# Moving half of the modulation products and the gate broadcasts of a two-layer diffusion block into the stretches between its projections

## What is computed

```python
for l in range(2):
    sh1, sc1, gt1, sh2, sc2, gt2 = split(silu(c) @ w_mod[l] + b_mod[l], 6)      # w_mod[l]: 1024 x 6144
    csh1, csc1, cgt1, csh2, csc2, cgt2 = the same of c_ctx
    h = rms_norm(x, g_pre_mix[l]) * (1 + sc1) + sh1                             # hc likewise for ctx
    y, yc = token_mixer(h, hc, ...)       # @ w_in; differential attention; gated linear attention; @ w_out
    x = x + gt1 * rms_norm(y, g_post_mix[l])                                    # ctx too, in layer 0
    h = rms_norm(x, g_pre_ffn[l]) * (1 + sc2) + sh2
    x = x + gt2 * rms_norm(ffn(h), g_post_ffn[l])   # layer 0: dense SwiGLU, layer 1: 8 experts, top 2
```

## Time and profile before

| | |
|---|---|
| median of 3 runs | 2058.43 us (2058.36 to 2059.71) |
| the profiled execution's own time | 2058.17 us |
| its span | 2056.0 us |
| PE busy, DVE, ACT | 93%, 60%, 52% of the span |
| DMA | 441.87 MB, 215 GB/s on average |

### The profile page before, as it was taken

One profiled execution on the slowest core, in us unless ns is written; L12 is line 12 of the kernel. 1 busy time (PEld: TensorE's weight loads), 2 busy tenths in 40 slices (PEclk: granted clock), 3 DMA queues, 4 the chain that ended last, 5 costly groups with the idle time before them and its releaser, 6 DMA issues.

```text
span 2056.0 us, 25790 instructions
## 1 busy us (share of the span) xinstructions
PE 1911.4 (93%) x10392; PEld 1579.1 (77%) x10392; DVE 1243.5 (60%) x1379; ACT 1069.3 (52%) x1368; POOL 43.6 (2%) x38
## 2 busy tenths in 40 slices
PE   6999889979999998898887999999999999999995
PEld 4889456868888786788567788888888888888784
DVE  3241751452222334442654889898989898888886
ACT  4232642352222224433534677677777777676764
POOL 0000000000000000000000020000000000000000
PEclk9999885889999999899967899999999999999997
DMA  8211633212222222212802899998989998989894
GB/s 336 103 62 63 226 145 121 73 49 105 83 103 102 82 103 82 89 62 103 307 22 82 319 350 368 338 368 343 366 342 364 344 362 346 360 343 343 336 339 163
DMA packets 61530, 441.87 MB, mean 215 GB/s; under 512 B 6836, under 2 KB 6964, under 8 KB 8288
## 3 DMA queue, kind: packets, MB, share of 16 engines
q1 hardware_dynamic: 60032, 436.23, 56.3%
q10 hardware_dynamic: 1120, 3.28, 0.4%
q0 software_dynamic: 256, 0.66, 0.1%
HBM read 439.10 MB, written 1.05 MB: 214 GB/s over the span
## 4 chain that ended last, share of the span: by engine, by line
PE 84%; DVE 10%; ACT 3%; DMA 2%; issue 1%; SPq 0%; DVEq 0%; ACTq 0%
PE psum L1446 72%; DMA raw<-units 2%; PE psum L1782 2%; PE psum L1658 1%; PE psum L1664 1%; DVE act_lo L1088 1%; PE psum L1641 1%; PE psum L1825 1%; DVE row_max L1168 1%; PE psum L1463 1%; PE psum L1798 1%; ACT probs L773 1%; DVE states L1199 1%; PE psum L1469 1%; DVE y_mix L1237 1%
## 5 line engine op out<-in xcount | busy, mean ns | idle before, releaser
L1331 DVE TENSOR_TENSOR w_lo<-raw,w_hi 128x2048 fp32r<-128x2048 f32 x136 | 311.0, 2289 | 52.3 <-ACT w_hi L922 51.6
L922 ACT ACTIVATE w_hi<-raw 128x2048 fp32r<-128x2048 f32 x136 | 260.8, 1919 | 109.0 <-PE psum L1446 106.4
L1024 DVE TENSOR_TENSOR w_lo<-raw,w_hi 128x1024 fp32r<-128x1024 f32 x130 | 153.3, 1221 | 197.9 <-ACT w_hi L628 197.9
L1446 PE MATMUL psum<-w_hi,xt_hi 128*128 128x512 f32 x596 | 234.2, 393 | 2.7 <-DVE xt_lo L1336 2.7
L1446 PE MATMUL psum<-w_hi,xt_lo 128*128 128x512 f32 x596 | 233.4, 392 | 0.0
L1446 PE MATMUL psum<-w_lo,xt_hi 128*128 128x512 f32 x596 | 233.2, 391 | 0.0
L1331 DVE TENSOR_TENSOR w_lo<-raw_more,w_hi 128x2048 fp32r<-128x2048 f32 x90 | 206.0, 2290 | 35.7 <-ACT w_hi L922 35.3
L628 ACT ACTIVATE w_hi<-raw 128x1024 fp32r<-128x1024 f32 x130 | 130.2, 1051 | 157.2 <-PE psum L1446 151.6
L922 ACT ACTIVATE w_hi<-raw_more 128x2048 fp32r<-128x2048 f32 x90 | 172.8, 1920 | 75.4 <-PE psum L1446 75.4
L1446 PE MATMUL psum<-act_hi,w_hi 128*128 128x512 f32 (+1 forms) x544 | 208.8, 384 | 2.1 <-DVE act_lo L1088 1.9
L1446 PE MATMUL psum<-act_lo,w_hi 128*128 128x512 f32 (+1 forms) x544 | 207.6, 382 | 0.0
(11 more groups left out here) (260 smaller groups left out, 3636.1 us busy)
## 6 DMA issues: line engine op xcount, KB each, us to landing
raw<-units SPq DMA_DIRECT2D x295, 1024.0 KB, 4.9
raw_more<-units SPq DMA_DIRECT2D x120, 1024.0 KB, 4.9
X<-ctx_in ACTq DMA_DIRECT2D x1, 1024.0 KB, 16.6
X<-x_in ACTq DMA_DIRECT2D x1, 1024.0 KB, 23.3
out<-X SPq DMA_DIRECT2D x1, 1024.0 KB, 4.1
const<-const_in ACTq DMA_DIRECT2D x1, 520.0 KB, 9.6
rope<-rope_in POOLq DMA_DIRECT2D x2, 256.0 KB, 5.6
wsm<-wsm_in ACTq DMA_DIRECT2D x1, 288.0 KB, 26.9
```

Of the source, the lines that this page charges most:

```text
L922: act.activation(w_place(m)[0], raw_place(m), ACT.Copy).then_inc(esem("w_high"), 1)
L1024: ins = dve.tensor_tensor(w_lo[:, i % RING, part], raw[:, i % RING, part], w_hi[:, i % RING, part].bitcast(F32), ALU.subtract)
L1331: dve.tensor_tensor(lo, raw_place(m), hi.bitcast(F32), ALU.subtract).then_inc(esem("w_ready"), 1)
L1446: ins = pe.matmul(dst, lhs(a), rhs(b), start=first and n == 0, stop=last and n == 2)
```

## The change

The 48 modulation units keep their order by need, but 24 of them leave attention and GLA. Of layer 0's attention, units 20 to 23 go; units 0 to 7 of layer 1 leave GLA; all twelve go into the gap before the dense FFN. Of layer 1's attention, units 8 to 15 go into the gap before its input projection and units 20 to 23 into the gap after its output projection; units 16 to 19 stay, now with one step every item. `gap_places` lists the places in a gap: P (after a tile's squares of y), N (after a tile's squares of X), V, and, before the dense FFN only in effect, K (after column blocks 1, 3, 5, 7 of `modulated`). PE does the steps of the P, N and V places before the turn, those of K after the eight T jobs. Two projection units (`AHEAD`) are numbered before a gap's modulation units. The gate broadcasts w=0 move from before the output projection to behind it, those of w=1 to the end of the dense FFN (layer 0) and behind the turn (layer 1). The DVE split of the first output unit now falls into attention, as do ACT's splits of the first two. `residual` runs tile by tile with steps between, one tile behind the squares after a mixer and two behind after the FFN.

```diff
+MOD_GROUPS = {
+    ("mod_a", 0): [(0, j) for j in range(MOD_A)],
+    ("mod_att", 0): [(0, j) for j in range(MOD_A, 20)],
+    ("mod_ffn", 0): [(0, j) for j in range(20, MOD_UNITS)] + [(1, j) for j in range(MOD_A)],
+    ("mod_mix", 1): [(1, j) for j in range(MOD_A, 16)],
+    ("mod_att", 1): [(1, j) for j in range(16, 20)],
+    ("mod_ffn", 1): [(1, j) for j in range(20, MOD_UNITS)],
+}
+AHEAD = 2
+STAGES = (("mod_a", 0), ("in", 0), ("mod_att", 0), ("out", 0), ("up_ahead", 0), ("mod_ffn", 0), ("up", 0), ("down", 0),
+          ("in_ahead", 1), ("mod_mix", 1), ("in", 1), ("mod_att", 1), ("out", 1), ("mod_ffn", 1), ("moe", 1))
...
 def beside(l, stage):
-    if (l, stage) == (1, "gla"):
-        return {}
-    units, step = {(0, "att"): ([(0, j) for j in range(MOD_A, MOD_UNITS)], 2),
-                   (1, "att"): ([(1, j) for j in range(MOD_A, MOD_UNITS)], 1),
-                   (0, "gla"): ([(1, j) for j in range(MOD_A)], 2)}[l, stage]
-    return {n * step: here for n, here in enumerate(mod_steps(units))}
+    return {2 * n: here for n, here in enumerate(mod_steps(MOD_GROUPS["mod_" + stage, l]))}
+def gap_places(l, stage):
+    tiles = len(token_tiles(l, stage))
+    places = [("P", n) for n in range(tiles)] + [("N", n) for n in range(tiles)] + [("V", 0)]
+    places += [("K", k) for k in (1, 3, 5, 7)]
+    return dict(zip(places, mod_steps(MOD_GROUPS["mod_" + stage, l])))
+def gap_jobs(l, stage, behind):
+    return [key for place, here in gap_places(l, stage).items() if (place[0] == "K") == behind for key in here]
...
 # ACT, out_projection
+            gates_on_all(l, 0)
             act.wait_ge(sem(f"act_lo_out{l}"), KT)
-            mean_square("post", l, "mix", ...)
-            gates_on_all(l, 1)
+            for n in range(len(token_tiles(l, "out"))):
+                mean_square("post", l, "mix", ..., (n,))
+                gap(l, "ffn", ("P", n))
+        def normed(l, stage):
+            for n in range(len(token_tiles(l, stage))):
+                norm(l, stage, (n,))
+                gap(l, stage, ("N", n))
+            gap(l, stage, ("V", 0))
 # ACT, end of dense_ffn
             for t in range(TILES):
                 for h in range(2):
                     key = ("D", 0, t, h)
                     copy_out(key, y_ffn[:, t, h * 512:(h + 1) * 512], bank(key))
...
+                if t == 1:
+                    gates_on_all(0, 1)
+                if t:
+                    tile_square(t - 1)
+            tile_square(TILES - 1)
+            for n in range(TILES):
+                gap(1, "mix", ("P", n))
...
 # DVE
+        def residual_beside(l, stage, y, after):
+            tiles = len(token_tiles(l, "out"))
+            behind = 1 if stage == "mix" else 2
+            for n in range(tiles + behind):
+                if n >= behind:
+                    residual(l, stage, y, n - behind)
+                if n < tiles and stage == "mix":
+                    gap(*after, ("P", n))
+                elif stage != "mix" and n >= 2:
+                    gap(*after, ("P", n - 2))
+        def normed(l, stage):
+            for n in range(len(token_tiles(l, stage))):
+                gap(l, stage, ("N", n))
+                norm(l, stage, (n,))
+            gap(l, stage, ("V", 0))
...
 # PE
+            if l == 1:
+                gates_on_all(0, 1)
+                for key in gap_jobs(1, "mix", False):
+                    mod_step(*key)
             turn(l, "mix")
...
             gla(l)
+            out_projection(l)
             gates_on_all(l, 0)
-            out_projection(l)
-            gates_on_all(l, 1)
+            for key in gap_jobs(l, "ffn", False):
+                mod_step(*key)
             turn(l, "ffn")
+            for key in gap_jobs(l, "ffn", True):
+                mod_step(*key)
             if l == 0:
                 dense_ffn()
...
+        gates_on_all(1, 1)
         for q in range(4):
             key, tt = ("H2", q), q // 2
```

More of the change, by code:

```diff
@@ L60 @@
 EXPERT_UNITS = 3 * FC
[L64 to L67, removed]
+MOD_GROUPS = {
[9 more added lines that the diff above has]
+          ("in_ahead", 1), ("mod_mix", 1), ("in", 1), ("mod_att", 1), ("out", 1), ("mod_ffn", 1), ("moe", 1))
+STAGE_UNITS = {("in", 0): IN_F + IN_K, ("out", 0): OUT_UNITS, ("up_ahead", 0): AHEAD, ("up", 0): UP_UNITS - AHEAD,
+               ("down", 0): DOWN_UNITS, ("in_ahead", 1): AHEAD, ("in", 1): IN_F + IN_K - AHEAD, ("out", 1): OUT_UNITS,
+               ("moe", 1): EXPERTS * EXPERT_UNITS}
+STAGE_UNITS.update({stage: len(here) for stage, here in MOD_GROUPS.items()})
 def unit_numbers():
@@ L85, in split_numbers @@
     for stage in STAGES:
-        for i in range(STAGE_UNITS[stage[0]]):
-            if stage[0] not in ("mod_a", "mod_b"):
+        for i in range(STAGE_UNITS[stage]):
+            if stage not in MOD_GROUPS:
                 at[U[stage] + i] = n
@@ L110, in mod_unit, with in_unit, up_unit @@
 def mod_unit(l, j):
-    return U["mod_a", l] + j if j < MOD_A else U["mod_b", l] + j - MOD_A
+    return next(U[stage] + here.index((l, j)) for stage, here in MOD_GROUPS.items() if (l, j) in here)
+def in_unit(l, u):
+    return U["in", 0] + u if l == 0 else U["in_ahead", 1] + u if u < AHEAD else U["in", 1] + u - AHEAD
+def up_unit(j):
+    return U["up_ahead", 0] + j if j < AHEAD else U["up", 0] + j - AHEAD
 def mod_steps(units):
@@ L211, in psum_jobs @@
             out += [key for here in mod_steps([(0, j) for j in range(MOD_A)]) for key in here]
+        if l == 1:
+            out += [("GB", 0, 1, s, h) for s in sides(0) for h in range(2)]
+            out += gap_jobs(1, "mix", False)
         out += [("T", l, "mix", k) for k in range(KT)]
+        out += gap_jobs(1, "mix", True) if l == 1 else []
         out += [("F", l, f) for f in range(2 * IN_F)]
@@ L249, in psum_jobs @@
         else:
+            out += [("GB", 1, 1, s, h) for s in sides(1) for h in range(2)]
             out += [("H2", q) for q in range(4)] + [("LG",), ("POS",)]
@@ L658, in beside_item, with gap @@
                 mod_step(*key)
+        def gap(l, stage, place):
+            for key in gap_places(l, stage).get(place, ()):
+                mod_step(*key, ahead=0)
         def gates_on_all(l, w):
@@ L868, in dense_ffn, with tile_copied, tile_square @@
                 act.activation(ffn_hi[:, f % 2, :], ffnT[:, f, :], ACT.Copy).then_inc(sem("ffn_hi"), 1)
+            def tile_copied(n):
+                for h in range(2):
+                    wait_copied(act, ("D", 0, n, h))
+            def tile_square(t):
+                mean_square("post", 0, "ffn", range(TILES), y_ffn_of, lambda t: y_junk[:, :], tile_copied, (t,))
             for t in range(TILES):
@@ L1089, in low_parts @@
                                   ALU.subtract).then_inc(sem(f"act_lo_{stage}{l}"), 1)
+                if stage != "out" and (l, stage) != (0, "mix"):
+                    gap(l, stage, ("K", k))
         def in_projection(l):
@@ L1437, in _ @@
         dve.wait_ge(sem("summed"), 1)
-        residual(1, "ffn", y_moe_of)
+        for n in range(2):
+            residual(1, "ffn", y_moe_of, n)
     @block.tensor
```

113 lines of the change are left out of this document (54 added, 59 removed).

## The result

The kernel after takes 2073.47 us (median of 4 runs, 2072.95 to 2074.01) beside 2059.07 (4 runs, 2058.36 to 2062.63) for the kernel before on the same chip: ratio 1.0066, 95% interval 1.0049 to 1.0084. It is slower. The traces are compared by span, 2071.8 against 2056.0: 15.8 us to explain.

The account below looks back on a forecast made before the run. PE carried 84% of the chain of waits, but the five changed places had different limits. Against 2058.17 us: -18.9 + 1.7 + 15 + 15.5 - 11.8 + 0 + 5.5 = +7.0, 2065.2 us; range 2049 to 2077.

Parts of the forecast that it names:

- GLA 0: Layer 0's GLA loses eight modulation steps and falls from 70.2 to 51.3 us: -18.9 us.
- the first gap to its turn: Gap before the dense FFN, up to the turn: 26.5 us against 18.4, +8.1 us.
- Attention 0: Layer 0's attention loses four steps that cost nothing and gains output-unit splits: +1.7 us, between 0 and 4.7.
- half-clock branch: Gap before the dense FFN: at 1.2 GHz PE sets the pace, 2.95 us a step, 27.3 us to the turn.
- The same gap, behind the turn: Gap before the dense FFN, after the turn: products and column blocks take 13 us against 6.1, +6.9 us.
- Nothing changes behind the turn: After the turn before layer 1's input projection, up to attention 1: no change, 0 us.
- Gap before projection 1: Gap before layer 1's input projection: 31 us to the turn against 15.45, +15.5 us, bounds +12.5 and +18.5.
- Attention 1: Layer 1's attention: fewer steps an item give -15.6, splits return +3.8; -11.8 us, bounds -15.6 and -8.
- GLA 1 and output projection 1: Layer 1's GLA and output projection: moved split and removed broadcast give 0 us, bounds -2 and +3.
- Before the router: Gap before the router: turn moves about 2.9 us, w=1 broadcast adds 2 to 3.8; +5.5 us, bounds +2 and +7.
- Rival B: Gaps at half clock throughout, attentions slowed too: gaps +18, +18.5, +7, attentions +2; sum +16.5, 2074.7 us; chance 0.15.
- Rival A: PE keeps the upper clock (2.4 GHz) in the gaps, products at 1.07 us: -7.5, 2050.7 us; chance 0.25.

Follow-up runs that it names:

- v4: v3 with six of its twelve up-phase units moved before the FFN, three before input projection 1, three staying; 2041.4 us, ratio 0.9909.
- v6: v4 with FFN gates broadcast in the gap before the FFN, and six full-width fillers ahead of input projection 1's turn; 2039.0 us, ratio 0.9907.
- v3: Kernel after with sixteen units in attention 0, eight in attention 1, twelve plus FFN gates in the FFN's up phase, mixing gates early; 2054.0 us, ratio 0.9970.

## Why the prediction was right or wrong

I forecast +7.0 (2065.2) with slower as likeliest; it came out slower by 13.6 (ratio), inside the range, but nearly twice the forecast. Point by point:

- **GLA 0** was right to 0.1 us, and **the first gap to its turn** to 0.6 (+8.7 for +8.1). **Attention 0** came out at +1.6 for +1.7, but this stretch varies: the two runs with six and nine units, which don't touch it, have 91.3, or +0.4. In the gap the clock fell after four products and PE's 2.81 a step set the pace, as the half-clock branch had it.
- **"The same gap, behind the turn"** was mis-sized: 6.9 for 13.6. I had the six column blocks behind the first product go through without a break. In fact every second one hands its bank to a step, so the chain is copy, product, copy in turn: rounds of 3.1, 3.1 and 4.4 us, and the first FFN matmul comes at 17.6 instead of 13. That is +11.5 over the 6.1 of before; the other 2.1 are the FFN's first matmuls at half clock, a term that my sum lacked. The run without the products won 11 us. The whole gap, +22.3, lies above my upper bound of 18.
- **"Nothing changes behind the turn"** failed: +7.0, of which 3.6 are the stall by the slots and some 2.8 the halved clock behind it. I had counted when units are loaded, not when their split parts may be written. The runs with six and nine units show it.
- **Gap before projection 1**: +17.1 for +15.5, within its bounds, and ACT's first `mod_row` copy at 13.3 for 14. The run with no units there splits it: 9.5 for the units, and 7.6 that are there without them, 6.5 of them the gates' broadcasts ahead of the squares.
- **Attention 1** fell by 15.2 for 11.8, within its bounds. Of the splits for which I gave back 3.8, only DVE's lies in the chain, with 2.27 us (row below). The tail behind the last row maximum, which I had taken from layer 0 as 8.85, is 7.3 here; the items themselves were right to 0.4. The 1.15 for an item's second step was too low: 11.8 / 6 = 2.0 by the run that put twelve units back.
- **GLA 1 and output projection 1** -0.6 for 0 (-1.7 ahead of GLA, +1.1 behind its start). **Before the router** +2.8 for +5.5. **Rest** 0, as costed.
- **Rival B**'s 2074.7 is the nearest of the four numbers to the 2073.5 measured, and that is luck. It had the clock right in most of the gaps, but the second is the only gap whose term came near (+17.1 for its +18.5). The first was +22.3 for +18 and the router's +2.8 for +7; it had attention dearer than my forecast by 2 where attention 1 came out 3.4 cheaper, and it had nothing for the +7.0 behind the second turn.
- **Rival A** was wrong about this kernel. Products at 1.07 are to be had (six of the eight in one gap of the run with fillers), but the products' own work doesn't bring a fallen clock back. The rule on idle stretches that I drew on from the Trainium skill ("TensorE: Matmul & The Clock Gate", Why this matters for your kernels) doesn't suffice here: the window of the kernel after has no idle time in 12 us, and 0.50.

DVE's split in attention 1's chain, kernel after:

```profile
1013.95 2.27 DVE w_lo L1082 x2
```

By spans the misses of one sign (+6.7, +7.0, +1.6, and +2 in small ones) add up to 17 and those of the other (-3.4 in attention 1, -0.6, -2.7, and -1.5 in output projection 0) to 8. They cancelled to 8.8, and the time was in the range by this luck too.

## What to carry to other kernels

Idle time of an engine in a gap is worth only what the gap's own chain leaves: here ACT's order, PSUM banks and a halved clock made 24 units in 45 us of idle PE dearer than beside GLA. The first few units of a gap are cheap (six for 1.0 us in v4, where PE still waits 2.7 us ahead of the turn), the later ones 2 to 2.5 us each ahead of the turn and 3.6 behind the FFN's; the free places were one unit for each attention item, and 1.67 each in a stretch where PE is busy with full-width work. When loads of another kind are put into a ring, count the slot of every buffer that shares its number, not the raw one alone.

## What the runs showed of the hardware

- With modulation steps alone the granted clock was 0.50 while PE was busy 12.00 of 12 us; one filler of 128 by 256 columns ahead of each product, and the same window had 1.00. In the other gap, with the same fillers, the clock fell behind a wait of 2.06 us and stayed at 0.50 for 16 us of busy PE, to the turn.
- The clock came back in the middle of full-width work: within the turn of the kernel after (0.50 from 437 to 442, the product behind it at 1.07), and within six fillers of v6 (0.50 at 822, 0.96 from 823 to 824), where it was lost again at the start of the turn, behind 1.99 us of waiting.
- The clock also dips where nothing was edited. The first row maximum of attention 0 lies between 204.3 and 207.6 us in the traces of kernels with the same code before it. In the window below the kernel before has 1.00; the kernel after has:

```profile
138.00:144.00 6.00, 6.00 (x37) 5.81 (x37) 2.28 (x4) 5.71 (x10) 0.00 (x0) 0.72 0.00 0
```

  So differences of 3 us between single traces are not evidence. Stretches of a ledger are better, since they begin behind such a dip, but not free of it: with eight units before projection 1 and the same code, the turn to attention 1 takes 142.7 to 144.5 us, and v3 has a dip of its own there.
